# A two-block float32 transformer on one core: where split weight places turn, when the next weights are rounded, and the order at the end of retention

## The reference, cut to what matters

```python
def first_block(x, ...):
    for l in range(DEPTH):                                   # DEPTH = 2
        h = rms_norm(x, ffn1_norm[l])
        x = x + 0.5 * swiglu(h, ffn1_w_gate[l], ffn1_w_up[l], ffn1_w_down[l])   # 1024 -> 2816 -> 1024
        h = rms_norm(x, mix_norm[l])
        (..., bgate) = jnp.split(h @ w_in[l], SPLIT_POINTS, axis=-1)
        y_nsa, y_sb, y_swa = ...        # three attentions, the first with compressed keys
        g = jax.nn.sigmoid(bgate).reshape(B, S, 3, D_MODEL)
        merged = (g[:, :, 0] * (y_nsa @ w_up_nsa[l]) + g[:, :, 1] * (y_sb @ w_up_sb[l])
                  + g[:, :, 2] * (y_swa @ w_up_swa[l]))
        x = x + merged @ w_out[l]
        h = rms_norm(x, ffn2_norm[l])
        x = x + 0.5 * swiglu(h, ffn2_w_gate[l], ffn2_w_up[l], ffn2_w_down[l])
    return x

def second_block(x, c, ctx, c_ctx, ada_w, ada_b, ...):
    for i in range(DEPTH):
        mod_l = (silu(c) @ ada_w[i] + ada_b[i])[:, None, :]
        sh_a, sc_a, g_a, sh_m, sc_m, g_m = jnp.split(mod_l, N_MOD, axis=-1)
        h_l = modulate(rms_norm_2(x, norm_mix_g[i]), sh_a, sc_a)
        y_l = even_mixer(...) if i % 2 == 0 else retention_mixer(...)
        x = x + g_a * y_l
        x = x + g_m * sq_relu_mlp(modulate(rms_norm_2(x, norm_mlp_g[i]), sh_m, sc_m), mlp_w1[i], mlp_w2[i])
    return rms_norm_2(x, final_g)

def merge(o_f, o_b, g_f, g_b):          # the end of retention_mixer
    y = silu(g_f) * head_rms(o_f) + silu(g_b) * head_rms(o_b)
    return y @ w_out
```

## Time and profile before

| | |
|---|---|
| runs of the kernel | 2577.38, 2578.32, 2583.74 us (median 2578.32) |
| the profiled execution, its own time | 2579.67 us |
| its span | 2577.9 us |
| mean granted clock of TensorE | 0.981 of full speed |
| PE busy | 2492.8 us (97%), 18069 matmuls |
| DVE busy | 1617.8 us (63%) |
| ACT busy | 1193.7 us (46%) |
| POOL busy | 335.3 us (13%) |
| read from HBM | 394.72 MB |

### The profile page before, as it was taken

How to read it: one execution, slowest core, us unless ns; L and a number is a source line. 1 busy time by engine, 2 the same in 40 slices (tenths; PEclk the granted TensorE clock), 3 DMA queues, 4 the chain that set the end, 5 groups by cost and what they waited for, 6 DMA issues and landing times.

```text
span 2577.9 us, 42373 instructions
## 1 busy us (share of the span) xinstructions
PE 2492.8 (97%) x18069; PEld 2323.6 (90%) x18069; DVE 1617.8 (63%) x2446; ACT 1193.7 (46%) x1958; POOL 335.3 (13%) x372
## 2 busy tenths in 40 slices
PE   8999989999999999899999999999999999999998
PEld 7999978999999899889999776888888999999998
DVE  4777566787888864667776776543443664555753
ACT  5444466544444355555545453431332544344653
POOL 1321000332022010022322000100001011001000
PEclk9999999999999999999999999999999999999999
DMA  7667544566766765336777220323233333334552
GB/s 235 209 213 206 155 158 116 163 222 229 241 222 220 234 177 177 115 115 229 255 262 219 66 62 17 98 98 94 86 98 98 125 98 115 99 99 148 164 197 99
DMA packets 386386, 401.67 MB, mean 156 GB/s; under 512 B 44695, under 2 KB 370611, under 8 KB 385940
## 3 DMA queue, kind: packets, MB, share of 16 engines
q1 hardware_dynamic: 383448, 391.19, 48.6%
q10 hardware_dynamic: 2748, 7.76, 0.8%
HBM read 394.72 MB, written 4.19 MB: 155 GB/s over the span
## 4 chain that ended last, share of the span: by engine, by line
PE 77%; DVE 15%; ACT 5%; issue 2%; DMA 1%; POOL 1%; DVEq 0%; SPq 0%; ACTq 0%
PE bank L672 23%; PE bank L673 22%; PE bank L674 22%; DVE rounded L2380 6%; PE bank L680 4%; DVE plain L2369 3%; ACT rounded L1619 2%; PE bank L685 1%; PE bank L1555 1%; POOL plain L3438 1%; PE bank L1087 1%; PE bank L1117 1%; DVE plain L2504 0%; PE bank L780 0%; DMA plain<-in_ada_w 0%
## 5 line engine op out<-in xcount | busy, mean ns | idle before, releaser
L672 PE MATMUL bank<-rounded 128*128 128x256 f32 (+1 forms) x3704 | 1121.2, 303 | 21.9 <-DVE rounded L2380 17.8
L673 PE MATMUL bank<-rounded 128*128 128x256 f32 (+1 forms) x3704 | 1103.5, 298 | 0.0
L674 PE MATMUL bank<-rounded 128*128 128x256 f32 (+1 forms) x3704 | 1102.8, 298 | 0.0
L2380 DVE TENSOR_TENSOR rounded<-plain,rounded 128x1024 fp32r<-128x1024 f32 (+1 forms) x630 | 736.8, 1216 | 522.4 <-ACT rounded L1619 522.1
L672 PEld LDWEIGHTS bank<-rounded 128*128 128x128 f32 x3704 | 718.4, 194 | 57.5 <-DVE rounded L2380 20.4
L1619 ACT ACTIVATE rounded<-plain 128x1024 fp32r<-128x1024 f32 (+1 forms) x630 | 616.8, 1032 | 329.2 <-PE bank L674 288.5
L673 PEld LDWEIGHTS bank<-rounded 128*128 128x128 f32 x3704 | 718.6, 194 | 16.1
L674 PEld LDWEIGHTS bank<-rounded 128*128 128x128 f32 x3704 | 718.2, 194 | 16.5
L672 PE MATMUL bank<-rounded,rounded 128*128 128x256 f32 (+2 forms) x1472 | 454.2, 309 | 19.3 <-DVE rounded L2380 16.9
L674 PE MATMUL bank<-rounded,rounded 128*128 128x256 f32 (+2 forms) x1472 | 450.6, 306 | 0.0
L673 PE MATMUL bank<-rounded,rounded 128*128 128x256 f32 (+2 forms) x1472 | 449.9, 306 | 0.0
(11 more groups left out here) (305 smaller groups left out, 1975.6 us busy)
## 6 DMA issues: line engine op xcount, KB each, us to landing
plain<-in_mlp_w SPq DMA_DIRECT2D x64, 1024.0 KB, 5.3
plain<-in_ada_w SPq DMA_DIRECT2D x48, 1024.0 KB, 5.4
plain<-in_ffn_w_gate SPq DMA_DIRECT2D x44, 1024.0 KB, 5.8
plain<-in_ffn_w_up SPq DMA_DIRECT2D x44, 1024.0 KB, 5.8
plain<-in_ffn_w_down SPq DMA_DIRECT2D x32, 1024.0 KB, 5.3
plain<-in_w_in SPq DMA_DIRECT2D x32, 1024.0 KB, 5.7
plain<-in_od_w_in SPq DMA_DIRECT2D x32, 1024.0 KB, 5.7
plain<-in_ffn_w_down SPq DMA_DIRECT2D x16, 768.0 KB, 5.2
```

The source lines that it names most:

```text
L672: pe.matmul(dst, a[0], b[0], start=first and i == 0, stop=False)
L673: pe.matmul(dst, a[0], b[1], start=False, stop=False)
L674: ins = pe.matmul(dst, a[1], b[0], start=False, stop=last and i == n - 1)
L2380: dve.tensor_tensor(low, raw, top, SUB).then_inc(*done(("lo", m, half)))
```

## The change

Six edits, none of which changes what is computed.

1. **Split places.** A split unit takes the place given by its number among the split units, modulo 3, where it was its number among all units. `before(m)` is then the third split unit back.
2. **Feed-forward.** On ACT and DVE both next units are rounded at a block's head, before the block's products and SiLU. In the down part the next unit is rounded before the residual.
3. **Modulation.** The table ADA is spread evenly.
4. **Mixer.** PE: `gate(1)` goes ahead of `compress(1,1)`, the compressed values' matmuls behind `gate(2)`, `gate(4+2i)` and `third(i)` ahead of `compressed(0)`; the up-projection waits only for the bank of the last job (`free ao`), and the first block of `wo` takes k-tile 7 before 6. ACT and DVE follow that order; the table of exp is preloaded, most `lo(bg+3)` on DVE come one job later, and POOL merges seven tiles, DVE one.
5. **Odd, on PE.** The last `ones512` matmul stands inside the first block of `wo`, and k-tiles 12 to 15 of that block come after the first half of the next block.
6. **Odd, elsewhere.** The low part of tiles 0 to 11 moves from POOL to DVE, and the roundings of `wo` on ACT go ahead.

```diff
-ADA = {"a0": [7, 11, 15, 19, 22, 24, 26, 28], "b0": [1, 5, 9, 13, 17, 20, 22, 24, 26, 28, 30, 32],
+ADA = {"a0": [7, 10, 13, 16, 19, 22, 25, 28], "b0": [1, 4, 6, 9, 12, 15, 17, 20, 23, 26, 28, 31],
...
     def part(self, m, k, c0, n=128):
-        o = SPLIT + 4096 * (m % AHEAD) + k * self.units[m][3] + c0
+        o = self.slot(m) + k * self.units[m][3] + c0
...
+    def slot(self, m):
+        return SPLIT + 4096 * (self.split_turn[m] % AHEAD)
     def before(self, m):
-        m -= AHEAD
-        while m >= 0 and self.units[m][2] != "split":
-            m -= AHEAD
-        return m if m >= 0 else None
+        n = self.split_turn[m] - AHEAD
+        return self.split_units[n] if n >= 0 else None
@@ PE, mixer @@
         gate(0)
+        gate(1)
         compress(1, 1)
         keyfactors()
-        gate(1)
...
+            gate(4 + 2 * i)
+            third(i)
             if i == 0:
                 compressed(0)
-            gate(4 + 2 * i)
-            third(i)
@@ PE, up-projection @@
-                for x in new(at(s, "attended", "dve")):
+                for x in new(at("free", s, "ao", n - 1)):
                     pe.wait_ge(*x)
@@ ACT, feed-forward (DVE likewise, with lo) @@
             hi(U[s, "g", blk] + 3)
             fill(s, 2 * blk)
+            hi(U[s, "u", blk] + 3)
+            fill(s, 2 * blk + 1)
             for j in range(2):
...
-            hi(U[s, "u", blk] + 3)
-            fill(s, 2 * blk + 1)
@@ ACT, mixer @@
+        act.activation(M.spare, M.epsc, ACT.Exp, bias=0.0, scale=1.0).then_inc(*done())
...
+        weights(0)
         gate(2)
-        weights(0)
...
+        hi(U[s, "w1", 1, 1] + 3)
         headroot("kc", 15)
-        hi(U[s, "w1", 1, 1] + 3)
@@ POOL, merges of the mixer @@
-        for o in range(6):
+        for o in range(7):
@@ PE, odd @@
+        for j in range(2):
+            for k in range(8):
+                if (j, k) == (1, 5):
+                    headpower(3, 1)
+                ins = outer(0, k, j, bs[0][j])
@@ DVE, odd (removed on POOL) @@
+                if h == 3 and d == 1:
+                    for c in (0, 4, 8):
+                        for x in new(at(s, "yh", c)):
+                            dve.wait_ge(*x)
+                        dve.tensor_tensor(b_.Yl[:, c:c + 4, :], b_.Y[:, c:c + 4, :], b_.Yf[:, c:c + 4, :], SUB)
```

More of the change, by code:

```diff
@@ L231, in __init__ @@
         self.plan()
+        self.split_units = [m for m, u in enumerate(self.units) if u[2] == "split"]
+        self.split_turn = {m: n for n, m in enumerate(self.split_units)}
     def piece(self, tensors, o, n):
@@ L1126, in mixer @@
         gate(2)
+        values_compressed()
         headsum("kc", 15)
@@ L1162, in mixer @@
             if blk == 0:
-                for k in range(8):
+                for k in (0, 1, 2, 3, 4, 5, 7, 6):
                     for x in new(at(s, "M", k)):
@@ L1499, in gate, with headpower @@
             ins.then_inc(*done((s, "g", h, d, half), ("unit", m)))
+        def headpower(h, d):
+            b = bank(s, "n", h, d)
+            for x in new(at(s, "ss", h, d)):
+                pe.wait_ge(*x)
+            pe.matmul(b[:, 0:256], M.ones512, b_.sqb[:, 0, :], start=True, stop=True).then_inc(*done((s, "n", h, d)))
         for h in range(4):
@@ L1559, in odd @@
                     gate(h, *gates.pop(0))
-                b = bank(s, "n", h, d)
-                for x in new(at(s, "ss", h, d)):
-                    pe.wait_ge(*x)
-                pe.matmul(b[:, 0:256], M.ones512, b_.sqb[:, 0, :], start=True, stop=True).then_inc(*done((s, "n", h, d)))
-        for blk in range(4):
-            bs = [bank(s, "wo", 2 * blk + j) for j in range(2)]
-            for k0 in range(0, 16, 8):
-                m = U[s, "wo", blk, k0]
-                ready(m)
-                for j in range(2):
-                    for k in range(k0, k0 + 8):
-                        for x in new(at(s, "yk", k)):
-                            pe.wait_ge(*x)
-                        ins = product(bs[j][:, 0:256], [(part(m, k - k0, j * 128), (b_.Yr[:, k, :], b_.Yl[:, k, :]))],
-                                      k == 0, k == 15)
-                    keys = [("unit", m)] if j else []
-                    ins.then_inc(*done((s, "wo", 2 * blk + j, k0), *keys))
+                if (h, d) != (3, 1):
+                    headpower(h, d)
@@ new lines, in outer @@
+        def outer(blk, k, j, b):
+            m = U[s, "wo", blk, k // 8 * 8]
+            ready(m)
+            for x in new(at(s, "yk", k)):
+                pe.wait_ge(*x)
+            return product(b[:, 0:256], [(part(m, k % 8, j * 128), (b_.Yr[:, k, :], b_.Yl[:, k, :]))], k == 0, k == 15)
+        bs = [[bank(s, "wo", j) for j in range(2)], None, None, None]
+        for j in range(2):
[3 more added lines that the diff above has]
+                ins = outer(0, k, j, bs[0][j])
@@ new lines, in odd @@
+        ins.then_inc(*done((s, "wo", 0, 0), (s, "wo", 1, 0), ("unit", U[s, "wo", 0, 0])))
+        for j in range(2):
+            for k in range(8, 12):
+                outer(0, k, j, bs[0][j])
+        for blk in range(1, 4):
+            bs[blk] = [bank(s, "wo", 2 * blk + j) for j in range(2)]
+            for j in range(2):
+                for k in range(8):
+                    ins = outer(blk, k, j, bs[blk][j])
+                keys = [("unit", U[s, "wo", blk, 0])] if j else []
+                ins.then_inc(*done((s, "wo", 2 * blk + j, 0), *keys))
+            for b, k0 in ((0, 12), (1, 8)) if blk == 1 else ((blk, 8),):
+                for j in range(2):
+                    for k in range(k0, 16):
+                        ins = outer(b, k, j, bs[b][j])
+                    keys = [("unit", U[s, "wo", b, 8])] if j else []
+                    ins.then_inc(*done((s, "wo", 2 * b + j, 8), *keys))
@@ L1946, in mixer @@
         gate(0)
+        gate(1)
         hidden(1)
-        gate(1)
         headsq("kc", M.bank(s, "kc")[:, 0:15], 15, ("kc",))
-        for x in new(at(s, "vc")):
-            act.wait_ge(*x)
-        act.activation(b_.vc[0:15, :, :], grid(M.bank(s, "vc")[0:15, 0:128], c=2), ACT.Copy, scale=1.0).then_inc(
-            *done((s, "vc", "s"), ("free", s, "vc")))
+        act.activation(M.spare, M.epsc, ACT.Exp, bias=0.0, scale=1.0).then_inc(*done())
         def compressed(step):
@@ L1973, in mixer @@
         n = len(b_.jobs)
+        weights(0)
         gate(2)
-        weights(0)
+        for x in new(at(s, "vc")):
+            act.wait_ge(*x)
+        act.activation(b_.vc[0:15, :, :], grid(M.bank(s, "vc")[0:15, 0:128], c=2), ACT.Copy, scale=1.0).then_inc(
+            *done((s, "vc", "s"), ("free", s, "vc")))
+        hi(U[s, "w1", 1, 1] + 3)
         headroot("kc", 15)
-        hi(U[s, "w1", 1, 1] + 3)
         gate(3)
@@ L2001, in mixer @@
         for blk in range(4):
-            for j in range(2):
+            for j in (1, 0) if blk == 3 else (0, 1):
                 o = 2 * blk + j
@@ L2315, in odd @@
                         square(s, o, at(s, "x", o), 0, 256, M.two.sq)
-                if not (blk == 3 and k0 == 8):
-                    hi(U[s, "wo", blk, k0] + 3)
         here("end", s, "act")
```

69 lines of the change are left out of this document (38 added, 31 removed).

## The result

| | before | after |
|---|---|---|
| median | 2579.97 us (8 runs) | 2558.49 us (7 runs) |
| ratio, 95% interval | | 0.9918 [0.9895, 0.994] |
| profiled execution, its own time | 2579.67 us | 2553.16 us |
| span | 2577.9 us | 2551.4 us |

An eighth run of after took 3422.28 us at a mean granted clock of 0.649 and is left out (with it the median would be 2561.68); the others lie between 2550.62 and 2568.21. The kernel is faster, by 0.8%, where 2.2% was forecast. 2558.49 lies outside the range of 2502 to 2552, and the gain is 21 of the 57 us of the sum, or 26 of them in the profiled execution.

A forecast was written before the change was run, and what follows sets the result against it. PE was taken to bound the kernel, so time is saved where it waits: 30 us (feed-forward), 20 (mixers) and 7 (odd) make 57, from 2579.67 to 2522.7, written as 2522 us; range 2502 to 2552.

The forecast's parts named there:

- Feed-forward, the size of the gain: Stages a0, b0, a1, b1, edits 1 to 3: 30 us less, bounds 0 and 34.5.
- What the products lose is 2.4 us of earliness ... I cost both at nothing: Feed-forward blocks: products come 2.4 us later; work behind them and banks freed later were both costed at nothing.
- a ring that comes round in three blocks or so: Feed-forward: PE's banks, freed 2.4 us later, are reused only after about three blocks, so the delay costs nothing.
- The removed waits: Feed-forward: 28.5 us of PE waits go, low-part waits falling from 26.8 to under 6; 34.5 with half clock.
- the 2.4 us piece of DVE's idle time: Feed-forward, sign of being right: DVE's idle time ended by ACT's rounding no longer has this piece in each block.
- The places: Feed-forward, edit 1: the split place comes free no later than before; no gain of its own was counted.
- The table: Feed-forward, edit 3: spreading ada units keeps DVE's average under PE, though a full block has 11.9 us against 11.5.
- the products wait in line: Rival, feed-forward: a held rounding also holds products, SiLU and banks in 44 blocks; 2595 us, chance 0.05 (slower).
- DVE stays the limit: Rival, feed-forward: blocks with a full ada unit overload DVE, 11.9 us against 11.5; 2537 us, chance 0.15.
- POOL and DVE hold each other up: Rival, feed-forward: POOL's SiLU multiplies hold DVE for their length, 0.74 us each; 2545 us, chance 0.11.
- Mixers and odd: Mixers, edit 4: 20 us for both, 5.8 up-projection and 4.3 middle in each; odd's end, edits 5 and 6: 7 us.
- the sum comes no sooner: Odd's end: DVE's sum of squares takes 4.5 us against 4.4; PE's 39 matmuls, 4.7 us, cover the wait instead.

The follow-up runs named there:

- the repaired kernel: Kernel after with modulation reductions behind the products, a0's first two blocks in old order, down-part residual first, three ADA steps changed: 2520.87 us.
- the repaired kernel of 2522.77 us: Kernel after with modulation reductions behind the products, a0's first two blocks in old order, down-part residual first; ADA table as after: 2522.77 us.
- the one of the mixer's middle: Kernel after with compressed(0) ahead of gate(4) and third(0) on PE, as before the change: 2564.17 us.

## Why the prediction was wrong

**Feed-forward, the size of the gain: wrong.** The step that failed is "What the products lose is 2.4 us of earliness ... I cost both at nothing". The edit moved not a low part but a low part and the filling of its step, and the filling is an ada unit and up to two turns: 6.5 us between the low parts and the first product in b0. I had listed the fillings in the sum for DVE's load, 11.9 us a block, and left them out of the order. The load was no limit: b1 ran with PE busy for 198 of 198 us. The second half of the step, "a ring that comes round in three blocks or so", held for blocks alone; a turn takes two banks more and a step of the relative bias four, and there the ring comes round in one block. Not nothing, then, but 19.4 us of waits for products' banks, and in a0 a granted clock of 0.94 in place of 0.97.

**The removed waits: right.** Those for low parts fell to 3.5, under the 6 stated, in b1 to nothing, for which I had kept back 2.7. That they were worth about 34.5 is shown by the repaired kernel. One sign failed all the same: the 2.4 us piece of DVE's idle time is still there (2.41 at 626.53, above), and before the low parts DVE is idle for 511.7 us in all, against 522.4. It ends earlier now, and PE no longer waits for what follows it.

**The places: wrong.** "The split place ... comes free no later than before" is true and missed that with the old numbering it comes free later than the new order needs it (20 us).

**The table: right that it moves no load, wrong that spacing is all it does.** In the new order the even table was no better than the old one. What mattered is the parity of the steps at which a chunk ends, which the table and the code of the turns show.

**The rival "the products wait in line"** had the right mechanism and the wrong place and price. It expected the rounding to be held, by a late transfer or a late place, in all 44 blocks. The products were held in three blocks and at a0's head, behind DVE's own work, which took back 19.4 us of waits and their half clock, where the rival had counted 44 us.

**"DVE stays the limit" and "POOL and DVE hold each other up"**: neither happened. POOL's multiplies have a median of 0.74 us as before, and DVE's low parts a mean of 1.22 (1.223 against 1.216), some 4 us more over all 630. The rule about the shared port in the Trainium skill (SBUF — State Buffer, "SBUF: two separate sides") agrees with L3347's two operations, 4.33 us beside POOL and 0.76 without; but as the products come last in a block, most multiplies fall beside the products or in DVE's wait for the next rounding (2.4 us at 624.1 to 626.5). They do meet an ada unit's operations at times, as they did before: 9 of the 88 multiplies take over 1 us, up to 1.73, each beside a multiply or multiply-add of 128x1024; before it were 11, up to 1.59.

**Mixers and odd: sizes near, for the mixers in part by luck, one reason wrong.** 19 us for 20, and 6.5 for 7. In the mixers PE's idle time fell by 11 us of the 19; the other 8 are clock, and not the same in every execution (last section). The merges on POOL cost two waits, 1.1 us in a mixer, where 0.4 was kept back. The gain at the up-projection was put to the new mark, and belongs to DVE's new order, with its last `lo(bg+3)` behind the old one. In odd, "the sum comes no sooner" was wrong by about 2 us: before, DVE had waited 1.91 us for ACT's squares ahead of L3304, and the subtractions fill that time.

## What to carry to other kernels

- When a call that issues work is moved in a queue that runs in order, list everything that the call issues at each of its steps, the rare cases first. Here 24 waits of 3.5 us at most were removed, and most of it was given back in the few blocks where the moved call issued 6.5 us of work besides its 2.4, and where a bank ring that was long enough for the common block was too short.
- Look at waits by what they are for, not by their sum: the old wait was gone as planned, and the new one named the line that had been moved.
- Of edits that come together, take each one back alone: here the rest was worth nothing without one that was costed at nothing, and the one meant to carry the gain cost time as it was made.

## What the runs showed of the hardware that I had not expected

The same code ran at different clocks from one execution to the next. The even mixer is word for word the same in all kernels, and PE's waits in it are alike. Its rows in the repaired kernel of 2522.77 us and in the one of the mixer's middle:

```profile
1332.00:1587.00 255.00, 245.78 (x1392) 193.92 (x1392) 166.19 (x360) 117.19 (x245) 12.71 (x15) 0.99 0.23 71
```
```profile
1372.00:1637.00 265.00, 255.99 (x1384) 198.29 (x1383) 165.86 (x358) 116.78 (x244) 12.26 (x14) 0.94 0.22 67
```

10 us more at a granted 0.94 instead of 0.99. Half and more of it is one stretch of small matmuls behind the last attention job, in the first of these kernels and in the second:

```profile
1497.00:1510.00 13.00, 13.00 (x32) 5.52 (x31) 4.22 (x7) 5.28 (x7) 0.00 (x0) 1.00 0.04 12
```
```profile
1537.00:1550.00 13.00, 13.00 (x22) 5.46 (x21) 7.26 (x12) 3.00 (x6) 0.00 (x0) 0.50 0.26 81
```

PE is busy throughout in both, and at half clock, 1.2 GHz, in the second. In the runs of after the mean granted clock goes with the time: 0.985 in the one of 2550.62 us, 0.977 in that of 2568.21. So a difference of less than 10 us between two profiles in a stage of small matmuls says nothing by itself, and the 4 us by which the even mixer was longer after the change are of this kind.

So is a part of the mixers' gain. The kernel with the `ones512` matmul put back has the first-block mixer of after, and its m0 took 5 us more than after's 252, at the clock of before:

```profile
251.00:508.00 257.00, 251.12 (x2018) 236.37 (x2017) 165.92 (x334) 149.11 (x295) 29.02 (x32) 0.95 0.51 147
```

PE's idle time there is 5.9 us, against 12.7 in m0 of before: that the waits went is shown, and at the same clock they are worth 5 us in a mixer. The 22 mixers of the eleven kernels that share this code took 249 to 257 us, 253.5 on average, so 8 to 9 less than the 262 of the one trace of before. Whether the shorter waits also make the better clock likelier, these runs don't show. A stage of large matmuls without waits did not vary (b1: 198.1 us in after and ten of the twelve kernels).
